# Two routing heads of the first chunk made late, and six VectorE additions moved to TensorE

## The reference, cut to what matters

```
q = (xc @ w_q).reshape(128, 8, 2, 128)                     # 8 heads, two halves
sc = einsum('chid,hikd->chik', q, sub_keys)                # 128 keys a half
top_s, top_i = top_k(sc, 16);  cand = sums of all pairs;  best_s, best_c = top_k(cand, 16)
expert = i1 * 128 + i2;  gate = softmax(best_s)
u_e, v_e = u_tab[expert], v_tab[expert]                    # 16 rows of each a head and token
act = gelu(einsum('chkd,cd->chk', u_e, xc))
x = x + einsum('chk,chkd->cd', gate * act, v_e)
```

## Time and profile before

| | us |
|---|---|
| median of 3 runs | 1693.49 (1692.49 to 1695.54) |
| the profiled execution: its own time | 1692.46 |
| its span in the trace | 1690.5 |
| PE busy | 1544.3 (91%) |
| DVE busy | 1159.9 (69%) |
| ACT busy | 742.4 (44%) |
| POOL busy | 584.7 (35%) |
| moved by DMA | 675.13 MB, mean 399 GB/s |

### The profile page before, as it was taken

One profiled execution on the slowest core, in us unless ns is written; L12 is line 12 of the kernel. 1 busy time (PEld: TensorE's weight loads), 2 busy tenths in 40 slices (PEclk: granted clock), 3 DMA queues, 4 the chain that ended last, 5 costly groups with the idle time before them and its releaser, 6 DMA issues.

```text
span 1690.5 us, 19142 instructions
## 1 busy us (share of the span) xinstructions
PE 1544.3 (91%) x6354; PEld 896.5 (53%) x6354; DVE 1159.9 (69%) x2898; ACT 742.4 (44%) x2021; POOL 584.7 (35%) x527
## 2 busy tenths in 40 slices
PE   9999999899999999988999889988999999777776
PEld 8757775347567656434645446434656554232232
DVE  7821799974877558886555667995556666666655
ACT  4142534763464333485433353465444334333333
POOL 0000444443323334343333343243333444343331
PEclk9999999999999999999999999999999999999999
DMA  9639899999999999999999999999999999999997
GB/s 384 259 127 358 329 416 421 415 421 420 420 421 396 421 421 421 420 421 421 421 421 421 421 418 420 409 417 402 421 411 417 421 421 421 421 421 421 421 422 293
DMA packets 94003, 675.13 MB, mean 399 GB/s; under 512 B 10424, under 2 KB 10704, under 8 KB 12496
## 3 DMA queue, kind: packets, MB, share of 16 engines
q0 software_dynamic: 73728, 536.90, 76.8%
q1 hardware_dynamic: 20032, 136.74, 19.9%
q10 hardware_dynamic: 144, 0.26, 0.0%
HBM read 672.81 MB, written 1.05 MB: 399 GB/s over the span
## 4 chain that ended last, share of the span: by engine, by line
PE 44%; DMA 29%; ACT 6%; DVE 5%; issue 2%; POOL 0%; ACTq 0%; POOLq 0%
DMA slots<-expert_rows,expert 29%; PE bank L1011 24%; PE bank L481 9%; PE bank L684 3%; DVE slots L2045 3%; PE bank L978 2%; PE bank L994 2%; ACT diag L1530 1%; ACT coef L1552 1%; ACT L1547 1%; PE bank L771 1%; PE bank L749 1%; DMA ring<-w_blocks 1%; ACT gel L1547 1%; PE bank L540 0%
## 5 line engine op out<-in xcount | busy, mean ns | idle before, releaser
L1011 PE MATMUL bank<-slots,diag 128*128 128x512 f32 x1914 | 906.9, 610 | 124.5 <-ACT diag L1530 117.7
L1152 POOL DMA_INDIRECT slots<-expert_rows,expert x512 | 582.8, 1138 | 1081.7 <-PE bank L1011 870.6
L2045 DVE CUSTOM_DVE_ANT_0 slots<-slots,htok 128x1024 f32<-128x1024 f32 x512 | 625.7, 1222 | 369.7 <-DMA slots<-expert_rows,expert 368.8
L1011 PEld LDWEIGHTS bank<-slots,diag 128*128 128x128 f32 x1914 | 348.1, 193 | 541.3 <-issue 326.3
L1547 ACT ACTIVATE gel<-dot 128x2 f32<-128x2 f32 (+1 forms) x258 | 52.4, 203 | 605.9 <-DVE dot L2045 605.4
L481 PEld LDWEIGHTS bank<-hT,ring 128*128 128x128 f32 x1440 | 173.8, 192 | 41.3 <-issue 39.9
L481 PE MATMUL bank<-hT,ring 128*128 128x128 f32 x1440 | 174.8, 275 | 1.3 <-ACT hT L1188 1.0
L1530 ACT ACTIVATE diag<-ident,coef 128x128 f32<-128x128 f32 x479 | 168.1, 394 | 8.4
L1552 ACT ACTIVATE coef<-gel,gexp 128x1 f32<-128x1 f32 x512 | 123.1, 287 | 10.4
L1547 ACT ACT_TABLE_LOAD x67 | 86.0, 1283 | 1.2
L1579 DVE SCALAR_TENSOR_TENSOR sg<-pad,prm,sg 128x128 f32<-128x128 f32 x240 | 71.5, 342 | 0.0
(11 more groups left out here) (363 smaller groups left out, 1473.2 us busy)
## 6 DMA issues: line engine op xcount, KB each, us to landing
ring<-w_blocks SPq DMA_DIRECT2D x89, 1024.0 KB, 9.2
slots<-w_blocks SPq DMA_DIRECT2D x24, 1024.0 KB, 13.9
slots<-expert_rows,expert POOLq DMA_INDIRECT x512, 15.5
kept<-w_blocks SPq DMA_DIRECT2D x4, 1024.0 KB, 15.5
keys<-w_blocks SPq DMA_DIRECT2D x2, 1024.0 KB, 10.4
kv<-w_blocks SPq DMA_DIRECT2D x2, 1024.0 KB, 13.8
prm<-small SPq DMA_DIRECT2D x2, 768.0 KB, 12.7
x<-x_rows SPq DMA_DIRECT2D x2, 512.0 KB, 11.3
```

The source lines that it names most:

```text
L1011: last = mm(bank[h][:, :], diag[:, i % DIAGS, :], slots[:, SLOT[n], D + h * 512:D + (h + 1) * 512], start=m == 0, stop=n == end - (ph == N ...
L1152: nc.gpsimd.indirect_dma_start(slots[:, s, :], None, (experts0_d, experts1_d)[n // PER // NC], bass.IndirectOffsetOnAxis(ap=idx[q % 2][:, ...
L2045: v.tensor_tensor_reduce(out=slots[:, s, 0:D], in0=slots[:, s, 0:D], in1=htok[:, ph % 2, :], scale=1.0, scalar=0.0, op0=ALU.mult, op1=ALU.add,
```

## The change

Heads 4 and 5 of stage 0 leave `HEADS[0]` and are made in `late_queries` of stage 1, at ticks 143 and 159, beside heads 6 and 7 (ticks 175 and 191), which were late already. Of stage 1's late heads, 4 and 7 are now transposed anew, and 5 and 6 use what was transposed for 4 (before: 6 and 7). The loads of both w_q blocks stay where they were in SP's order. The routing on DVE of head 1 starts three ticks later; that of heads 4 and 5 starts seven ticks later and takes two steps a tick instead of one. Their softmax on ACT no longer scales by `rs0`, since their tokens come normalized; it takes one short copy more (`nbest`). Among the first 16 experts, 2, 4, 7, 10, 12 and 15 were added by DVE and are now summed by PE.

```
-HEADS = [[0, 1, 2, 3, 4, 5], [7, 0, 6, 1, 4, 2, 5, 3], [0, 1, 2, 3, 4], [7, 0, 1, 2, 6, 5, 3, 4]]
+HEADS = [[0, 1, 2, 3], [7, 0, 6, 1, 4, 2, 5, 3], [0, 1, 2, 3, 4], [7, 0, 1, 2, 6, 5, 3, 4]]
-WQ_AT = [[89, 91, 93, 95, 103, 105], [94 + i * 5 // 2 for i in range(8)],
+WQ_AT = [[89, 91, 93, 95], [94 + i * 5 // 2 for i in range(8)],
...
-    return h == late_heads(ci)[0][0] or ci == 1
-
-
-TAKER = ["vector" if (n < 16 or 104 <= n < 144) and n % 8 in (2, 4, 7)
+    return h == late_heads(ci)[0][0] or (ci, h) == (1, PH - 1)
+
+
+TAKER = ["vector" if 104 <= n < 144 and n % 8 in (2, 4, 7)
...
+            for j in [j for j in issue if order[j][0] == 0 and WIDE <= spots[j][0] < WIDE + STAY]:
+                issue.remove(j)
+                issue.insert(next(i for i, k in enumerate(issue) if second[k]), j)
...
     if q == 1:
-        return 97 + n * 3 // 4
+        return G0 + (n - 1) * 3 // 4
```

## The result

| | before | after |
|---|---|---|
| median of 14 runs each, us | 1691.74 (1689.33 to 1695.54) | 1694.66 (1694.05 to 1697.93) |
| span of the profiled execution | 1690.5 | 1692.7 |
| moved by DMA | 675.13 MB | 675.12 MB |

The ratio is 1.0018 (95% interval 1.0011 to 1.0025): a little slower, by some 3 us, where 1.7 us faster was forecast. It lies inside the range of 1687.0 to 1697.5, and just inside the 0.2% that I called the same, but on the wrong side. One run of those reported further down, with expert 10 alone moved, took 2237 us at a mean granted clock of 0.67 and is left out of its ratio.

The account below looks back on a forecast made before the run. Bound: DMA's bytes at some 421 GB/s plus the time DMA has too little to do. Span 1690.5 - 2.5 + 0.8 = 1688.8 us, profiled execution 1690.8, median 1.0 above: 1691.8 us; range 1687.0 to 1697.5.

Parts of the forecast that it names:

- The step that failed: Gathers: landing time beyond 5.8 us is reserve, 2.5 us at the tightest of 220 to 230 us.
- First term: Ticks 102 to 118, first experts: earlier slots put transfers ahead, limited by gather 20's reserve; -2.5 us, bounds 0 and -5.8.
- nearly all of the 5.8: 190 to 215 us: the 5.8 us DMA loses there is nearly all won by 215 us.
- my rule: At gather 20, transfers can be at most 2.5 us earlier; the rest of the gain is given back at 220 to 232 us.
- Second term: Ticks 139 to 148: late head 4 makes experts 43 and 44 later on PE; +0.8 us, middle of 0 and 1.7.
- rival (b): Ticks 139 to 148: expert 40 not earlier, PE waits another 2 us for copies; +4 us, 1697.5 us, chance 0.14.
- Head 5 and the routing: Head 5's 4.2 us on PE near 352 to 362 us and the late routing of both heads cost nothing.
- reserve of over 11: Gathers from 340 us on have over 11 us in hand, against 2.5 us if routing were a tick late.
- rival (a): First experts: all the gain is kept, DVE's 7.7 us less work helping; -3.5 to -5.8 us, about 1688.9, chance 0.23.
- Rival (c): PE's clock: experts 6 and 7 run at the lower level, 3.5 us more before expert 13; 1694.5 us, chance 0.09.
- The Trainium skill's estimate: Lone gather: 2.0 us plus bytes at 436 GB/s, 4.4 us; reserve 3.9, sum -3.1 instead of -1.7; not adopted.

Follow-up runs that it names:

- head 5 only: The kernel before with head 5 alone made late, head 4, the six additions and head 1's routing as before; 1690.91 us, ratio 0.9993.
- old route: heads only with head 1's routing on DVE at its old ticks, three earlier; 1691.32 us, ratio 0.9997 to the kernel before.
- ten alone: The kernel before with expert 10 alone moved from DVE to PE; 1693.97 us, ratio 1.0010.
- two back: The changed kernel with experts 12 and 15 back on DVE; 1693.93 us, ratio 1.0009 to the kernel before.
- heads only: The changed kernel with experts 2, 4, 7, 10, 12 and 15 back on DVE; 1689.87 us, ratio 0.9987 to the kernel before.
- softmax later: heads only with ACT's softmax of heads 4 and 5 written two ticks later; 1690.04 us, ratio 0.9989 to the kernel before.
- softmax and vector: softmax later with experts 42 and 44 also added by DVE; 1689.98 us, ratio 0.9989 to the kernel before.

## Why the prediction was wrong

**The step that failed** is in the first part: "What exceeds about 5.8 us is queue: the reserve by which a slot may come later before DMA runs dry." 5.8 us is what a lone gather takes. But a lone gather does not fill the DMA engines: 1.05 MB in 5.8 us are 181 GB/s. Gather 7 of before, issued at 191.54 and landed at 197.18, shows it (columns as in the earlier trace rows):

```profile
191.50:193.00 1.50, 1.50 (x15) 1.50 (x15) 1.50 (x5) 1.23 (x3) 1.02 (x1) 1.00 0.16 66
194.50:196.00 1.50, 1.50 (x14) 1.39 (x13) 1.50 (x3) 0.00 (x0) 0.45 (x1) 1.00 1.01 426
196.00:197.50 1.50, 1.50 (x15) 1.50 (x15) 0.07 (x2) 0.89 (x2) 1.19 (x2) 1.00 0.24 93
```

For 1.5 us almost nothing moves, then the bytes go, then it is quiet again before the landing. Those gaps must be filled by other gathers. To move 421 GB/s, one must land every 2.49 us, and the runs show how many have to be under way. Over 156 stretches of 5 us (200 to 235 and 310 to 340 us, twelve executions: all but head 5 only and old route, whose traces lack over a fifth of the landings; four others lack about a tenth, taken as their neighbours'), counted from POOL's issues and landings:

| gathers in flight | stretches | median GB/s | lowest to highest |
|---|---|---|---|
| under 2.5 | 25 | 329 and 339 (under and over 2) | 239 to 395 |
| 2.5 to 3 | 22 | 387 | 352 to 424 |
| 3 to 3.5 | 31 | 419 | 323 to 436 |
| over 3.5 | 78 | 418 to 421 | 338 to 431 |

A landing of 8.4 us at 2.49 us each is 3.4 in flight. That was the state of before at 220 to 230 us (8.3 to 10.0) and nearly that at 310 to 320 (8.6 to 9.9): full rate, and nothing in hand. The table alone doesn't say what is cause, since a low rate and few gathers go together either way; ten alone and two back do, where experts were made later by the edit and the rate fell, with landings of 6.8 and 7.3 us at least. Why it takes about three is open: at 5.8 us each, 2.3 in flight would already give one every 2.49 us.

**First term, -2.5 us forecast, +1.0 measured** by 300 us (+0.4 in the second profile). The schedule was right: expert 13 at 224.42 for 224.1, and gather 20 lands at 232.5 where it had landed at 234.6, 2.1 us earlier. Two things were wrong. I took the gather with the shortest landing for the one that decides. But gathers 15 to 20 are issued over 18.8 us (207.78 to 226.58), 3.76 us apart, and 2.49 are needed; before, they were 3.07 apart. And I took the next gathers as covered, whose landing was 8.8 to 14.5 us. They came up to 2.5 us later (237.64 for 235.15, gather 25). The gain by 215 us was also smaller than "nearly all of the 5.8": the front stood at +3.5 and +4.1. By my rule that would not have mattered, since it still exceeds the 2.5 that gather 20 allows. But from 215 to 240 us 3.7 and 4.4 us were given back, and the front was at -0.2 and -0.3 instead of +2.5.

**Second term, +0.8 forecast, 1.9 to 3.6 measured** between 300 and 340 us. Two things failed here. Expert 43 came 4.2 us later (320.66 for 316.45), not 2.2 to 2.8: the two halves took what was forecast, but expert 40, forecast 1.4 us earlier because the front would be ahead, came 0.8 later, and PE's wait for ACT grew from 1.93 to 2.91 us. And the reserve was not there, by the same error: 4.2 us less the 3.3 that I had in hand would have cost 0.9. (I had taken the median landing for this place and the shortest for the first, without a reason.) That expert 40 was not earlier is the condition of rival (b), "the front's gain was lost at 220 to 232". Its sum did not come: PE does not wait for the copies between 312 and 323 us, it is ACT that waits 1.78 us for PE at 318.03, and against the medians measured side by side the kernel is 2.9 us slower, not 4.

**Head 5 and the routing, forecast nothing, 0.7 to 1.5 us measured** between 340 and 380 us. I costed the late routing by the gather that needs its experts, and never by the softmax that waits for it: it is written one tick behind the top 16, and ACT waits there with a gelu in its queue. The "reserve of over 11" was used up by that wait and by head 5's halves together.

**The rest.** DVE's 7.7 us less bought nothing, as rival (a) would have needed. Rival (c) did not come: experts 6 and 7 took 3.70 us together at 200.24, at full clock (1.00 in 195 to 205 us). Its 1694.5 us is nearest of all to the 1694.66 measured, and that is luck. The 1.1 to 2.6 us that the changed kernel has over before at 500 to 540 us were in no step. In the changed kernel PE does not wait behind that softmax; why, I did not settle. Summed to 1600 us, the front of the changed kernel is at -3.3 and -2.8 in its two profiles, whose spans are 2.2 and 3.0 us longer; the first lost 1.8 of it between 1000 and 1300 us, where nothing was changed, and before again lost 1.3 there. A small slip of reading: slice 27 of the earlier trace rows, with 417 GB/s, belongs to the full ones. The Trainium skill's estimate ("DMA: Bandwidth & Descriptors", "Anatomy of one DMA"), 4.4 us for a lone gather, would have made the reserve larger still; no gather of these runs landed in under 5.3 us.

## What to carry to other kernels

Where gathers feed DMA, the reserve is not landing time less that of a lone transfer. It starts at the number in flight that keeps the full rate, here about three to three and a half, and it is spent by every transfer of a stretch whose slots come slower than DMA takes them, not by the tightest one. Work moved to an engine that is full there is paid about one for one (six experts: 10.3 us moved, 9.9 of front lost by 300 us; one: 1.72 moved, 1.8 lost between 215 and 240), however idle the engine it comes from. And when a computation is made later, look for each instruction that waits for it and for what stands behind that instruction: the softmax held a gelu, and the gelu held TensorE. The best versions here, about 0.12% under before, keep the late heads and leave the six additions alone.

## What the hardware showed that I had not expected

DMA's busy share hides lost rate: in the changed kernel 215 to 235 us has a share of 0.94 and 352 GB/s, 84% of the 421 that it reaches at 1.01. The worst part of it, with about two gathers under way:

```profile
220.00:222.50 2.50, 2.50 (x14) 1.69 (x13) 2.50 (x7) 1.61 (x6) 1.58 (x1) 1.00 0.71 243
```

The clock of TensorE can make the same program differ by 2 us of front at 215 us: three experts in one piece took 5.42, 6.96 and 7.11 us in three executions (heads only, softmax later, softmax and vector), behind the same wait of 1.77 us. Gather 7 went out at 189.05, 190.67 and 190.82, and the front at 215 us was +5.2, +2.9 and +3.1. A lateness at one engine need not last, though: that of the slow first experts in two back was gone by expert 8. The runs of one kernel spread over 2 to 7 us here.

POOL's issue of a gather takes 0.94 us mostly, but up to 3.08. In the trace of before, 84 of the 512 take over 1.5 us, and 82 of these end 0.75 to 1.1 us after one of DVE's dot products or full additions ends; of the 325 that take under 1 us, 38 do. It looks as if the issue is held until DVE is through. No run here tests that, and I had it in no sum: in two back it made gather 21 later by over 2 us more than the moved expert did.
